# A one-core hybrid layer pair in float32: recurrence scores of two levels in one run of TensorE

## The reference

```python
def step(state, inp):                      # chunks of 64 tokens
    qc, kc, vc, gc = inp
    b = jnp.cumsum(gc, axis=2)             # log decay
    diff = b[:, :, :, None, :] - b[:, :, None, :, :]
    decay = jnp.exp(jnp.where(causal[None, None, :, :, None], diff, -jnp.inf))
    scores = jnp.einsum('bhtd,bhsd,bhtsd->bhts', qc, kc, decay)
    o_intra = jnp.einsum('bhts,bhsv->bhtv', scores, vc)
    o_inter = jnp.einsum('bhtd,bhdv->bhtv', qc * jnp.exp(b), state)
```

## Time and profile before

| | |
|---|---|
| median of three timed runs | 3679.75 us (3678.6 to 3681.87) |
| the profiled execution | 3675.55 us, its span 3673.8 us |
| granted TensorE clock, mean | 0.998 of full |
| PE busy | 3620.4 us |
| VectorE, ScalarE, GpSimd busy | 2044.2, 1505.4, 684.9 us |
| first and last score matmul | 35.5 and 1179.0 us |

### The profile page before, as it was taken

How to read it: one execution, slowest core, us unless ns; L and a number is a source line. 1 busy time by engine, 2 the same in 40 slices (tenths; PEclk the granted TensorE clock), 3 DMA queues, 4 the chain that set the end, 5 groups by cost and what they waited for, 6 DMA issues and landing times.

```text
span 3673.8 us, 62759 instructions
## 1 busy us (share of the span) xinstructions
PE 3620.4 (99%) x25576; PEld 3121.9 (85%) x25576; DVE 2044.2 (56%) x3869; ACT 1505.4 (41%) x2733; POOL 684.9 (19%) x405
## 2 busy tenths in 40 slices
PE   8999999999999999999999999999999999999999
PEld 6889888978897988987788778888877899998998
DVE  4757635551545354556645665555566565546555
ACT  3332431231232364576565665444555422223222
POOL 2001130000000000233333321000000254415442
PEclk9999999999999999999999999999999999999999
DMA  7756687567655877866766665554533666666664
GB/s 300 281 182 245 242 291 262 195 217 236 224 219 187 287 255 245 286 233 220 259 229 228 218 237 183 166 169 148 174 139 120 228 247 239 234 232 228 233 234 183
DMA packets 215534, 820.57 MB, mean 223 GB/s; under 512 B 22096, under 2 KB 71504, under 8 KB 152144
## 3 DMA queue, kind: packets, MB, share of 16 engines
q1 hardware_dynamic: 215248, 816.57, 63.6%
HBM read 615.15 MB, written 201.33 MB: 222 GB/s over the span
## 4 chain that ended last, share of the span: by engine, by line
PE 93%; DVE 3%; ACT 2%; issue 1%; POOL 0%; DMA 0%; SPq 0%; DVEq 0%; ACTq 0%; POOLq 0%
PE bank L1615 89%; PE bank L1619 4%; DVE P L2835 0%; DVE SH L2517 0%; ACT L2223 0%; DVE Z1a L2485 0%; SPq L3090 0%; DVE R L2438 0%; ACT slot L2107 0%; DVE P L2791 0%; DMA KS<-Kd 0%; DVE P L2841 0%; POOL SF L3031 0%; ACT P L2224 0%; ACT TP L2243 0%
## 5 line engine op out<-in xcount | busy, mean ns | idle before, releaser
L1615 PE MATMUL bank<-slot,Z0b 128*128 128x512 f32 (+1 forms) x3504 | 703.1, 351 | 0.8 <-DVE R L2438 0.4
L1615 PEld LDWEIGHTS bank<-slot,Z0b 128*128 128x128 f32 x3504 | 559.8, 188 | 91.2 <-DVE R L2438 2.1
L1615 PE MATMUL bank<-Z1a,slot 128*128 128x512 f32 (+1 forms) x2568 | 607.7, 381 | 13.5 <-DVE slot L2373 9.4
L1615 PE MATMUL bank<-Z1b,slot 128*128 128x512 f32 (+1 forms) x2568 | 608.3, 380 | 5.3 <-DVE Z1b L2485 5.3
L1615 PEld LDWEIGHTS bank<-Z1a,slot 128*128 128x128 f32 x2568 | 448.1, 190 | 103.0 <-DVE slot L2373 9.4
L1615 PEld LDWEIGHTS bank<-Z1b,slot 128*128 128x128 f32 x2568 | 444.2, 189 | 94.2 <-DVE Z1b L2485 7.3
L3046 POOL TENSOR_TENSOR slot<-raw,slot 128x1024 fp32r<-128x1024 f32 x110 | 273.4, 2492 | 706.8 <-ACT slot L2107 706.6
L2438 DVE SCALAR_TENSOR_TENSOR R<-bank,small,R 128x512 f32<-128x512 f32 x352 | 261.1, 747 | 176.1 <-PE bank L1615 175.7
L2791 DVE TENSOR_SCALAR_CACHE_REDUCE P<-bank 128x512 f32<-128x512 f32 (+3 forms) x320 | 189.2, 608 | 213.1 <-PE bank L1615 212.1
L1615 PE MATMUL bank<-KS,DQ 128*128 128x512 f32 (+3 forms) x960 | 277.9, 388 | 6.0 <-ACT P L2224 3.3
L3062 POOL TENSOR_TENSOR Z0b<-AF,Z0b 128x512 fp32r<-128x512 f32 x88 | 132.8, 1510 | 804.9 <-ACT Z0b L2297 804.8
(11 more groups left out here) (260 smaller groups left out, 5497.0 us busy)
## 6 DMA issues: line engine op xcount, KB each, us to landing
slot<-Wd SPq DMA_DIRECT2D x350, 1024.0 KB, 5.7
Wd<-slot SPq DMA_DIRECT2D x130, 1024.0 KB, 7.6
raw<-in_wts_dram SPq DMA_DIRECT2D x210, 512.0 KB, 4.6
DQ<-Qd SPq DMA_DIRECT2D x192, 128.0 KB, 4.2
slot<-Wd SPq DMA_DIRECT2D x40, 512.0 KB, 6.1
DV<-Vd SPq DMA_DIRECT2D x60, 256.0 KB, 4.7
KS<-Kd SPq DMA_DIRECT2D x24, 512.0 KB, 7.6
KS<-Kd SPq DMA_DIRECT2D x24, 384.0 KB, 7.2
```

The lines of the kernel that those rows point to most:

```text
L1615: return e.matmul(o, a, b, start=start, stop=stop, skip_group_check=True)
```

## The change

The scores of levels 2p and 2p + 1 are made in one run p (0 to 3). Both sets of queries and keys must then exist at once, so a second pair of buffers is used: new tiles Qc, and Fb, which is free after the first totals. Level 0 reads Qb and Kb, level 1 Qc and Kb, 2 Qc and Kb, 3 Qb and Fb, 4 the same, 5 Qc and Kb, 6 the same, 7 Qb and Fb. VectorE makes an odd level's decays in place and writes an even one's into the other buffers (hgrn_decayed); the halves that a level leaves as they are ScalarE copies over, two copies of 128x256 per half and run (L2154, L2155 of the new program), for runs 0 to 2. The product of queries with F stands before the first run now. The two levels' scores lie side by side in bank 2 + j, and the second half takes its two levels in turned order, so that equal tile sizes meet. The tile sg is dropped and its users take DG. The planner is given new costs, and its order shifts for all engines, beyond the recurrence into the first part of the attention.

```diff
-            t[j] = P.put(("hg k", u, j), ("dve", 1400))
-        for i, L in enumerate((0,) + LEVELS):
+            t[j] = P.put(("hg k", u, j), ("dve", 2100))
+        for p in range(4):
             x = max(t)
             yield x
             for j in range(2):
-                t[j] = P.put(("hg sc", u, i, j), ("pe", 400), after=x) + 200
+                t[j] = P.put(("hg sc", u, p, j), ("pe", 550), after=x) + 200
             for j in range(2):
                 yield t[j]
-                t[j] = P.put(("hg l", u, i, j), ("dve", 2200 if L == 16 else 1350 if L <= 16 else 1050), after=t[j])
+                t[j] = P.put(("hg l", u, p, j), ("act", 900), ("dve", (2500, 2500, 3300, 900)[p]), after=t[j])
         yield ("ev", ("A", s, 2 * hp, 1))
         for j in range(2):
...
+        def level_operands(i, j):
+
+            return (Qc if i in (1, 2, 5, 6) else Qb)[j], (Kb if i in (0, 1, 2, 5, 6) else Fb)[j]
+
+        def halves_of(b, L):
+
+            return b[:, :].rearrange("p (n two l) -> p n two l", two=2, l=L)
+
+        def level_scores(i, j):
+
+            w = 64 if i == 7 else 32
+            at = 128 * (i % 2)
+            return bank[2 + j][:, at:at + NT * w].rearrange("p (c t) -> p c t", c=NT)
 
...
-            def hgrn_scores(u, i, j):
-                L = ((0,) + LEVELS)[i]
-                A_ = bank[2 + j]
-                if i == 0:
-                    pe.wait_ge(*dve_hg("hg k", u, j, "k"))
+            def hgrn_scores(u, p, j):
+                if p == 0:
+                    pe.wait_ge(*dve_hg("hg k", u, j, "q"))
                     pe.wait_ge(*act_g("ev", ("A", u // 2, (24 if u % 2 else 6) + j)))
                     if u:
                         pe.wait_ge(*dve_hg("hg n", u - 1, j, "on"))
                 else:
-                    pe.wait_ge(*dve_hg("hg l", u, i - 1, j, "m" if i - 1 <= 5 else "q"))
-                    if i - 1 > 5:
-                        pe.wait_ge(*act_hg("hg l", u, i - 1, j))
-                for c in range(NT):
-                    if L <= 16:
+                    pe.wait_ge(*dve_hg("hg l", u, p - 1, j, "s" if p == 3 else "m1"))
+                    pe.wait_ge(*act_hg("hg l", u, p - 1, j))
+                for i in (2 * p, 2 * p + 1) if j == 0 else (2 * p + 1, 2 * p):
+                    q, k = level_operands(i, j)
+                    if i <= 5:
                         pairs = [(32 * g, 32 * g, 32) for g in range(4)]
                     else:
-                        pairs = [(0, 32, 32), (64, 96, 32)] if L == 32 else [(0, 64, 64)]
-                    for ks, qs, w in pairs:
-                        x = mm(A_[ks:ks + w, w * c:w * c + w], Kb[j][:, 128 * c + ks:128 * c + ks + w],
-                               Qb[j][:, 128 * c + qs:128 * c + qs + w], True, True)
-                x.then_inc(*pe_hg.inc("hg sc", u, i, j))
+                        pairs = [(0, 32, 32), (64, 96, 32)] if i == 6 else [(0, 64, 64)]
+                    for c in range(NT):
+                        for ks, qs, w in pairs:
+                            x = mm(level_scores(i, j)[ks:ks + w, c, :], k[:, 128 * c + ks:128 * c + ks + w],
+                                   q[:, 128 * c + qs:128 * c + qs + w], True, True)
+                x.then_inc(*pe_hg.inc("hg sc", u, p, j))
 
...
-            def hgrn_level(u, i, j):
-                if i <= 5:
+            def hgrn_level(u, p, j):
+                act.wait_ge(*pe_hg("hg sc", u, p, j))
+                if p < 3:
+                    i = 2 * p + 2
+                    act.wait_ge(*dve_hg("hg l", u, p, j, "u"))
+                    (q, k), (q1, k1) = level_operands(i, j), level_operands(i + 1, j)
+                    L = LEVELS[i - 1]
+                    e.activation(halves_of(q1, L)[:, :, 0, :], halves_of(q, L)[:, :, 0, :], ACT.Copy)
+                    e.activation(halves_of(k1, L)[:, :, 1, :], halves_of(k, L)[:, :, 1, :], ACT.Copy).then_inc(
+                        *act_hg.inc("hg l", u, p, j))
                     return
-                L = LEVELS[i - 1]
                 sv = heads_of(Sb[j])
-                act.wait_ge(*pe_hg("hg sc", u, i, j))
                 act.wait_ge(*pool_c("zero"))
                 if u:
                     act.wait_ge(*pe_hg("hg o", u - 1, j))
-                for r in (0, 64) if L == 32 else (0,):
-                    x = e.activation(sv[r:r + L, :, r + L:r + 2 * L],
-                                     bank[2 + j][r:r + L, 0:NT * L].rearrange("p (c t) -> p c t", c=NT), ACT.Copy)
-                x.then_inc(*act_hg.inc("hg l", u, i, j))
+                for i, L, r in (6, 32, 0), (6, 32, 64), (7, 64, 0):
+                    x = e.activation(sv[r:r + L, :, r + L:r + 2 * L], level_scores(i, j)[r:r + L, :, :], ACT.Copy)
+                x.then_inc(*act_hg.inc("hg l", u, p, j))
 
...
+                dve.wait_ge(*act_g("ev", ("A", s, (24 if hp else 6) + j)))
+                e.tensor_tensor(Qc[j][:, :], Qb[j][:, :], Fb[j][:, :], ALU.mult).then_inc(*dve_hg.inc("hg k", u, j, "q"))
+
+            def hgrn_decayed(u, i, j):
+
+                L = LEVELS[i - 1]
+                (q, k), (q1, k1) = level_operands(i, j), level_operands(i + 1 if i % 2 == 0 else i, j)
+                tl = tot(u, j, i - 1).rearrange("p (n two) -> p n two", two=2)
+                e.tensor_tensor(halves_of(q1, L)[:, :, 1, :], halves_of(q, L)[:, :, 1, :], bc(tl[:, :, 0], L, 2), ALU.mult)
+                e.tensor_tensor(tot(u, j, i), tl[:, :, 0], tl[:, :, 1], ALU.mult)
+                return e.tensor_tensor(halves_of(k1, L)[:, :, 0, :], halves_of(k, L)[:, :, 0, :], bc(tl[:, :, 1], L, 2), ALU.mult)
+
+            def hgrn_level(u, p, j):
+                dve.wait_ge(*pe_hg("hg sc", u, p, j))
+                if p:
+                    dve.wait_ge(*act_hg("hg l", u, p - 1, j))
+                hgrn_decayed(u, 2 * p + 1, j).then_inc(*dve_hg.inc("hg l", u, p, j, "u"))
+                if p == 3:
+                    return
+                dve.wait_ge(*dve_hg("hg l", u, p, j, "u"))
+                hgrn_decayed(u, 2 * p + 2, j).then_inc(*dve_hg.inc("hg l", u, p, j, "q"))
+                cv = Cb[j][:, :, :]
+                if p == 0:
+                    if u:
+                        dve.wait_ge(*dve_hg("hg l", u - 1, 2, j, "s"))
+                    dve.wait_ge(*d_c["pv"]("pv"))
+                    e.tensor_tensor(cv, level_scores(0, j), id4, ALU.mult).then_inc(*dve_hg.inc("hg l", u, p, j, "m0"))
                 else:
...
+                    dve.wait_ge(*act_c("lmask"))
+                    e.copy_predicated(cv, bc(lmask[:, 2 * p - 1, :], NT), level_scores(2 * p, j)).then_inc(
+                        *dve_hg.inc("hg l", u, p, j, "m0"))
+                dve.wait_ge(*act_c("lmask"))
+                dve.wait_ge(*dve_hg("hg l", u, p, j, "m0"))
+                e.copy_predicated(cv, bc(lmask[:, 2 * p, :], NT), level_scores(2 * p + 1, j)).then_inc(
+                    *dve_hg.inc("hg l", u, p, j, "m1"))
+                if p == 2:
+                    sv = heads_of(Sb[j])
+                    dve.wait_ge(*dve_hg("hg l", u, p, j, "m1"))
+                    dve.wait_ge(*pool_c("zero"))
                     if u:
...
+                        dve.wait_ge(*pe_hg("hg o", u - 1, j))
                     for g in range(0, 128, 32):
                         x = e.tensor_copy(sv[g:g + 32, :, g:g + 32], cv[g:g + 32, :, :])
...
+                    x.then_inc(*dve_hg.inc("hg l", u, p, j, "s"))
```

More of the change, by code:

```diff
@@ L1111, in build @@
         lamv = sb("lamv", [128, 8])
-        small = sb("small", [128, 512])
+        small = sb("small", [128, 360])
         raw = [sb(f"raw{i}", [128, 1024]) for i in range(NRAW)]
@@ L1306, in build @@
         act_hg = signal("act_hgrn", [x for st in order for x in (
[L1307 removed]
+            [st] if st[0] in ("hg kT", "hg l") else
             [st + (j, y) for y in ("ss", "sd") for j in range(2)] if st[0] == "hg n" else [])])
```

58 lines of the change are left out of this document (16 added, 42 removed).

## The result

| | before | after |
|---|---|---|
| median (lowest, highest; runs) | 3679.18 (3675.50, 3681.87; 4) | 3707.36 (3702.08, 3708.88; 4) |
| profiled execution, its span | 3675.55, 3673.8 | 3702.08, 3700.4 |

A forecast was written before the change was run, and what follows sets the result against it. PE, busy for 99% of the span, was taken as the bound. Terms: -9.0 + 1.9 + 5.8 + 3.0 - 1.8 + 1.5 = +1.4 us, forecast 3681 us, no change that can be told; range 3670 to 3692.

The forecast's parts named there:

- The saving: Score runs on PE: 32 merged runs instead of 64 remove 9.0 us in all, between 4.6 and 11.8.
- The step: Inside a score run on PE: each further load was put at 8.6 ns, 64 further steps at 0.55 us.
- the last pair: Merged run of levels 6 and 7, with tile size changes inside: 0.1 us saved for each of eight pairs.
- The rule of the Trainium skill: TensorE: a change of tiling mode, not tile alone, drains it; last pair then saves nothing, saving 8.2 instead of 9.0 us.
- The transposes of sub-blocks 1 and 2: Sixth and eighth unit: PE waits for VectorE's drains behind doubled levels, 2.9 us added twice, +5.8; bounds nothing and 4 each.
- The fourth unit and the pooling matmul: Sub-block 0's transposes: +3.0 us; pooling matmul at 471 us: wait goes or half stays, -1.8 us, bounds 0 and 3.6.
- the case that was priced at 3.8: Fourth unit's transposes: 3.8 us added if both halves' chain on VectorE must sit out GpSimd's weight split.
- The tile at 52 us: Weight tile split on ScalarE, behind the new copies: PE waits 1.9 us longer, bounds 0 and 3.
- Longer runs without gain: Rival: 128 small matmuls step slower on PE, a pair saves only 0.19 us; 3685.5 us, chance 0.08.
- Attention's start: Behind 1200 us: order shifts a little, waits may change by 3 us either way; inside the range.
- The lower clock: PE's clock may fall at three places with new waits of 2 to 3 us: +1.5 us, between 0 and 4.8.
- waits and the lower clock: Rival: PE stands still 2 to 4 us at three transpose places, clock falls each time: +9.5 us, 3689, chance 0.22.

The follow-up runs named there:

- e5: Changed kernel, but the recurrence of the fourth, sixth and eighth unit holds behind its first run until R's transposes are through: 3688.80 us, 1.0029 to before.
- e4: Changed kernel with ScalarE's copies of unscaled halves cut to their first block, output not the layer's: 3702.58 us, 1.0065 to before.
- e14: Changed kernel holding during R's transposes (fourth unit ahead of its first run), VectorE's levels in two stages in the first unit alone: 3681.53 us, 1.0009 to before.
- e7: Kernel before with every score matmul of the recurrence issued twice, 64 runs of 128: 3734.71 us, 1.0154 to before.
- e12: Changed kernel with eight 0.5 MB DRAM transfers added before the second and third run of the sixth and eighth unit: 3718.03 us, 1.0104 to before.
- e13: As e14, with large matmuls also between the halves of the runs of the third, fifth and seventh unit: 3677.46 us, 0.9994 to before.
- e1: Changed kernel, but attention waits in the plan until the same Q/K group as in the kernel before: 3699.74 us, 1.0050 to before.
- e3: Changed kernel with large matmuls between the halves of each merged run, so 64 runs of 64 score matmuls: 3693.79 us, 1.0039 to before.

## Why the prediction was wrong

Wrong by 26 us, and on the wrong side of its range. Step by step:

- **The saving**, forecast 9.0: measured 7.5. The step is 9.2 ns and not 8.6, and the last pair saves 0.07, not 0.1. A size, slightly off. Inside the last run the two changes of tile size take 0.27 us together: it lasts 1.70 from its first start to its last, where the two runs of before had 0.50 and 0.92. The rule of the Trainium skill that the prediction weighed (TensorEngine Tiling, Key Properties) agrees in that a change of mode costs time; that the pair saves nothing, as the prediction drew from it, did not come out.
- **The transposes of sub-blocks 1 and 2**, forecast +5.8: the chain was right. Waits went from 1.4 to 3.5 and 2.6 us, and with the clock these stretches cost 3.2 and 3.1 against before. e5 shows the cause.
- **The fourth unit and the pooling matmul**, forecast +3.0 and -1.8, measured +8.3 together (423 to 508 us). What failed is a path that the prediction left out. It followed VectorE's chain to the second pooling matmul alone: that wait went from 1.90 to 0.35, but in part by luck, since chain and PE were put at 9.4 and 11.3 us behind the first matmul and came at 14.1 and 13.8. The first pooling matmul, without a wait before and without a term in the sum, waited 4.28, since its chain started right behind two doubled levels and met GpSimd's split. The lower clock of this place, which was to go, stayed. And instructions ran short for 1.31. At the transposes the case that was priced at 3.8 came: VectorE's first product starts at 431.90, takes 1.76 and ends 0.3 us behind GpSimd's split.
- **The tile at 52 us**, forecast +1.9: the wait grew by 1.15, and the clock took up to 1.7 more. e4 and e14 put it on the copies and on their place in ScalarE's order.
- **What was not there at all**: instructions. "Longer runs without gain" asked whether the steps get slower; they don't, PE stops between blocks of its program. 5.5 us of idle time, and the clock at 350 us. Shown by e7 and e12. A wait for R of 1.08 behind the first of them may belong to it; that is not shown, for e13 has two like it, 1.06 and 1.07, with no such stop ahead of them.
- **Attention's start**, allowed for with 3 us either way: measured +9.6 (1206 to 1650 us), 5.5 of waits and up to 5.1 of clock. The planner's order for this stretch differed in 206 pieces, and I had called that "shifts a little". e1 and e5 bring back the waits of before behind 1262 us; the wait for the first keys stays between 0.6 and 4.1 us in all runs, and what sets it is left open.
- **The lower clock**, forecast +1.5 with at most 4.8: up to 13.6. It fell behind six waits of 2.2 to 2.8 us that had not been there, and each fall costs up to 1.7. This is the term that was most undersized, and it follows from the waits that were missed.

The rival "waits and the lower clock" had the mechanism, and its signs came: the transposes waited 2.73, 2.32 and 2.32 in one piece (in the fourth unit ahead of the fifth group, in the others of the eighth), and the idle time ahead of 1200 us grew by 16.8, over its 15. Its 3689 is still 18 under the measured time, since it stopped at three places.

## What to carry to other kernels

A merge that halves the fixed parts of a run doubles what stands behind it on the engine that works it up, and makes every place where that engine also frees banks for another stream a wait; look for these places first, and hold the stream back there. Follow the chain to every matmul that waits for that engine, not only to the one that waited before, and look at what GpSimd does beside it. Where an order is planned from costs, a change of work is also a change of order far behind it: diff the whole order, and price each stretch that differs. Before making runs of tiny matmuls longer, look at how full the DMA engines are there.

## What was not expected of the hardware

- PE can run out of instructions. Its program comes in packets of 16 KB, each taking 0.9 to 1.8 us in the changed kernel; runs of 128 matmuls and their loads use one up in about 1.2 us, and with the DMA engines at 0.80 or more PE stood still for 0.3 to 3.5 us, until 1.2 to 1.6 us behind the landing. With the engines under 0.80 it never did. e3 had two such stops inside runs of 64.
- It is not the same in every execution: at 350 us three kernels with one planned order up to there had 3.45, 2.32 and none.
- The clock and the waits that PE had before, over the 16 traces and without the first group: behind waits of over 4 us it went to the lower level every time (26 of 26, mostly for 6.8 us), behind 2 to 4 us in 68 of 105 (mostly for 3.4 us), behind 1.5 to 2 us in 20 of 59, behind 0.3 to 1.5 us in 13 of 318 (counted if the clock fell within 3 us of the wait's beginning).
- VectorE's first two pooling operations, 0.70 us each, took 2.86 and 2.75 beside GpSimd's splits of 1024 columns, and made most of a wait of 4.28 us.
